# Row factors of the shared key/value norm: from ScalarE's Ln and Exp with a Newton step on VectorE to a power on GpSimd

## The reference, cut to what matters

```python
def rmsnorm(x, g):
    xf = x.astype(jnp.float32)
    y = xf * lax.rsqrt(jnp.mean(xf * xf, axis=-1, keepdims=True) + RMS_EPS)
    return (y * g.astype(jnp.float32)).astype(x.dtype)

def shared_kv(x, norm_kv, w_kv):
    kv = rmsnorm(x, norm_kv) @ w_kv
    k, v = jnp.split(kv, [KV_WIDTH], axis=-1)
```

## Time and profile before

| what | value |
|---|---|
| median of 3 runs | 1838.86 us (1838.41 to 1840.55) |
| the profiled execution's own time | 1838.39 us |
| its span, first to last instruction | 1836.8 us |
| busy share of the span: PE, DVE, ACT, POOL | 95%, 61%, 48%, 14% |
| granted clock of TensorE, mean | 0.986 of full speed |

### The profile page before, as it was taken

How to read it: one execution, slowest core, us unless ns; L and a number is a source line. 1 busy time by engine, 2 the same in 40 slices (tenths; PEclk the granted TensorE clock), 3 DMA queues, 4 the chain that set the end, 5 groups by cost and what they waited for, 6 DMA issues and landing times.

```text
span 1836.8 us, 36758 instructions
## 1 busy us (share of the span) xinstructions
PE 1752.0 (95%) x14273; PEld 1369.2 (75%) x14273; DVE 1113.7 (61%) x2563; ACT 878.0 (48%) x1342; POOL 251.8 (14%) x350
## 2 busy tenths in 40 slices
PE   5999999999999999999999899999999999989996
PEld 4888876677677866677677777877778777778885
DVE  6535646574656546774767776466665676574443
ACT  6545542453343444544244665455555455464442
POOL 1112010131013011121013300210001101001110
PEclk7999999999999999999999999999999999999998
DMA  9423213552255314552254633332223322224432
GB/s 298 141 77 99 70 52 104 149 165 75 58 161 164 81 52 128 162 201 75 67 175 157 220 90 95 100 81 71 77 80 84 99 69 80 75 72 129 115 108 98
DMA packets 270600, 204.53 MB, mean 111 GB/s; under 512 B 8164, under 2 KB 254128, under 8 KB 269184
## 3 DMA queue, kind: packets, MB, share of 16 engines
q1 hardware_dynamic: 251200, 131.71, 25.9%
q0 software_dynamic: 19280, 71.13, 11.4%
HBM read 168.05 MB, written 38.80 MB: 113 GB/s over the span
## 4 chain that ended last, share of the span: by engine, by line
PE 84%; DVE 8%; ACT 3%; issue 2%; DMA 2%; SPq 0%; ACTq 0%; POOL 0%; DVEq 0%; POOLq 0%
PE PP L601 54%; PE PP L850 8%; PE PP L630 3%; PE BS L694 2%; PE B L1040 2%; PE B L725 1%; PE BS L754 1%; PE BS L504 1%; PE B L504 1%; DVE W L1812 1%; PE BS L997 1%; DMA W<-in_w_in_a 1%; PE PP L1133 1%; DVE AR L2042 1%; PE BS L752 1%
## 5 line engine op out<-in xcount | busy, mean ns | idle before, releaser
L601 PE MATMUL PP<-H,W 128*128 128x280 f16 (+1 forms) x8640 | 1055.1, 281 | 8.5 <-DVE W L1812 3.7
L601 PEld LDWEIGHTS PP<-H,W 128*128 128x128 f16 x8640 | 835.0, 98 | 197.7 <-issue 25.2
L1219 ACT ACTIVATE W<-W,SCL 128x1024 f16<-128x1024 f32 x240 | 262.7, 1139 | 333.4 <-DVE SCL L1746 318.8
L1812 DVE SCALAR_TENSOR_TENSOR W<-W,SCL 128x1024 f16<-128x1024 f32 x240 | 307.8, 1292 | 108.5 <-ACT W L1219 104.0
L1208 ACT ACTIVATE wjunk<-W 128x2048 bf16<-128x2048 f32 x120 | 227.7, 1897 | 22.7 <-DMA W<-in_w_in_a 11.0
L850 PE MATMUL PP<-O,W 128*128 128x280 f16 x1536 | 190.5, 284 | 4.8 <-DVE step L1743 4.1
L850 PEld LDWEIGHTS PP<-O,W 128*128 128x128 f16 x1536 | 148.0, 98 | 45.8 <-issue 11.9
L1589 ACT ACTIVATE AR<-AR 128x128 f32<-128x128 f32 x136 | 53.0, 391 | 87.1 <-DVE AR L2343 87.1
L601 PE MATMUL PP<-O,W 128*128 128x280 f16 x576 | 69.6, 282 | 0.5 <-DVE AR L2283 0.5
L1743 DVE TENSOR_SCALAR step<-PP 128x1 f32<-128x1 f32 x107 | 16.5, 154 | 85.3 <-PE PP L531 82.4
L504 PE MATMUL BS<-CST,AR 128*128 128x128 f32 (+3 forms) x318 | 48.4, 273 | 18.8 <-issue 6.5
(11 more groups left out here) (349 smaller groups left out, 1943.9 us busy)
## 6 DMA issues: line engine op xcount, KB each, us to landing
W<-in_w_in_a SPq DMA_DIRECT2D x48, 1024.0 KB, 6.0
W<-in_w_in_b SPq DMA_DIRECT2D x32, 1024.0 KB, 6.0
out<-AR POOLq DMA_DIRECT2D x36, 512.0 KB, 4.7
AR<-in_state_gla POOLq DMA_DIRECT2D x32, 512.0 KB, 5.7
W<-in_w_out_b SPq DMA_DIRECT2D x16, 1024.0 KB, 5.9
W<-in_w_out_a SPq DMA_DIRECT2D x16, 512.0 KB, 5.3
W<-in_w_out_a SPq DMA_DIRECT2D x32, 256.0 KB, 4.0
W<-in_w_kv SPq DMA_DIRECT2D x8, 1024.0 KB, 5.8
```

The source lines that it names most:

```text
L601: last = mm(PP[j % 2][:, c, 0:cols], w[:, k, :], x[:, c * cols:(c + 1) * cols], start=s_, stop=e)
L1219: A(w_parts(j % 2)[0][:, ks], W[:, j % 2, ks], ACT.Copy, scale=SCL[:, j % 4, 0:1]).then_inc(w_hi, 1)
L1812: STT(out=low[:, ks], in0=W[:, j % 2, ks], scalar=SCL[:, j % 4, 0:1], in1=high[:, ks], op0=ALU.mult, op1=ALU.subtract).then_inc(w_ready, 1)
```

## The change

GpSimd forms RB from acc itself, as a power with the exponent -1/2 taken from a column of `small` that DVE sets at the start. It does so in two instructions of 280 columns, each as soon as DVE has that half of acc. ACT's Ln and Exp go, and so do DVE's Newton step and the one-column copy. DVE no longer waits between the two halves of acc. It issues the first low half of the second key unit ahead of its wait for RB (before: between the first tiles of the pair) and then waits for both halves of RB.

```diff
-        ms_done, n_act, n_dve = sem("ms_done"), sem("n_act"), sem("n_dve")
+        ms_done, rb_root, n_dve = sem("ms_done"), sem("rb_root"), sem("n_dve")
...
-            def root(n):
-                act.wait_ge(n_dve, n + 2)
-                A(RB[:], acc[:], ACT.Ln).then_inc(n_act, 1)
-                act.wait_ge(n_act, n + 1)
-                A(RB[:], RB[:], ACT.Exp, scale=-0.5).then_inc(n_act, 1)
-
-            root(0)
             unit_high(kv_unit_at(1), 1)
...
+            V.memset(small[:, 67:68], -0.5)
...
             dve.wait_ge(ms_done, 1)
             cn = Tally(n_dve)
             for c_, b in enumerate((B0, B1)):
-                cn.link(dve, TS(acc[:, c_ * HALF:(c_ + 1) * HALF], b[:, 0:HALF], 1.0 / DM, EPS, ALU.mult, ALU.add))
-            cr = Tally(rs_dve, c.value)
+                cn.inc(TS(acc[:, c_ * HALF:(c_ + 1) * HALF], b[:, 0:HALF], 1.0 / DM, EPS, ALU.mult, ALU.add))
             unit_scale(kv_unit_at(1), 1, 1, B3[:, 300:301])
-            dve.wait_ge(n_act, 2)
-            newton(RB[:], acc[:], x2[:, 0, :], cr)
-            V.tensor_copy(small[:, 66:67], eps_c).then_inc(rb_ready, 1)
+            unit_low(kv_unit_at(1), 1, (0,))
+            dve.wait_ge(rb_root, 1)
+            dve.wait_ge(rb_ready, 2)
...
-                if n in (1, 5):
-                    unit_low(kv_unit_at(1), 1, (n // 5,))
+                if n == 5:
+                    unit_low(kv_unit_at(1), 1, (1,))
...
             residual(0, None, x1T, OUT_A3 // 2, TOK)
+            for c_, done in enumerate((rb_root, rb_ready)):
+                cols = slice(c_ * HALF, (c_ + 1) * HALF)
+                pool.wait_ge(n_dve, c_ + 1)
+                G.tensor_tensor(RB[:, cols], acc[:, cols], small[:, 67:68].broadcast_to([P, HALF]), ALU.pow).then_inc(done, 1)
+            pool.wait_ge(rb_root, 1)
             pool.wait_ge(rb_ready, 2)
             G.memset(acc[:], 0.0).then_inc(acc_zero, 1)
```

## The result

The changed kernel takes 1924.14 us (median of 4 runs, 1917.76 to 1925.31) against 1839.70 us (4 runs, 1838.41 to 1840.96): the ratio is 1.0453, 95% interval 1.0432 to 1.0475. It is 84 us longer, far above the range that ended at 1856 us.

What follows compares the result with a forecast made beforehand. The prediction took the ACT and DVE chain up to the pair's end as the bound, PE waiting for DVE's tiles. Change = 2T - 5.5 us = +0.9 us on 1838.86, so 1839.8 us; range 1835.5 to 1856 us.

Steps and rivals of the forecast that it cites:

- T: Time of one GpSimd power of 128 x 280, forecast at 3.2 us; it counts twice in the change.
- The bound above: Upper end for one GpSimd power of 280 columns: twice eleven passes at 0.69 us each, 15 us.
- geometric middle: Time of one GpSimd power taken as sqrt(0.69 x 15) = 3.2 us, between an add's time and 15 us.
- The third rival: GpSimd's power takes many passes, not overlapped: T = 15, about +25 us, 1864 us; T beyond 11 has chance 0.15.
- The blocking: GpSimd's power holds DVE off, so L1804 and the low half run after both powers: 1.20 + 0.2 us.
- Start: First GpSimd power starts 0.13 us after the first half of acc is done, at 1034.62 us.
- Release: GpSimd's release of DVE after the second power, ahead of the first `normed`: 0.10 us.
- The list: DVE's work from the first `normed` on gets one low half shorter: 1.20 us.
- The floor of 3.4 us: With a quick power, T under 1.75, the low half limits the first `normed`: change -3.4 us, 1835.5 us, chance 0.07.
- The 0 to 2 us: Extra time for PE's pair at half clock after idling, if the power is too slow: 0 to 2 us.
- Slower: Whole kernel slower by more than 0.2%: chance 0.28 + 0.15 = 0.43.

Runs made afterwards that it cites:

- the probes: The kernel before with seven powers that nobody reads, in the stretch where GpSimd waits for the value rows: ratio 1.0006.
- the run with T = 3.67: The changed kernel with the power on 17 of each half's 280 columns and a multiply on the other 263: ratio 0.9996 to the kernel before.

## Why the prediction was wrong

*The step that failed is T, "sqrt(0.69 x 15) = 3.2 us".* It measured 44.98 us, fourteen times as much. The bound above was the worse error: eleven passes for an inverse root, twice for a general power, each at the price of an add, was called a bound and was none. An add costs 0.69 us for 280 columns, so the power costs as much as 65 adds. No row of the trace of before held an operation near it, and a geometric middle between a floor and a guess then stood for knowledge. The third rival (many passes, +25 us at T = 15, a chance of 0.15 beyond T = 11) had the kind right and the size a third of it. The estimate from the Trainium skill (GPSIMD Engine Reference, Performance pitfalls for Q7 kernels), 73 ns a column, was nearer than mine and still less than half of the 160 measured; its 4 cycles a step and my 22 steps together don't account for what a column takes, and which of the two falls short no run here tells.

*The blocking was wrong as well, hidden under the first.* L1798 took 0.23 us and L1806 1.28 us under the first power, VectorE's two-input instructions ran at means of 793 and 739 ns beside the powers of the probes, and the run with T = 3.67 met the sum without the term. An add does hold a low half back: in the timeline of the kernel before, just behind the earlier trace rows, one that started under an add took 1.69 us instead of 1.28.

```profile
1004.34 1.69 DVE L1812 SCALAR_TENSOR_TENSOR W<-W,SCL 128x1024 f16<-128x1024 f32 x1
```

What this and the earlier trace rows show of an add does not hold for a power. So here the measurement speaks against the rule of the Trainium skill (SBUF — State Buffer, Who interferes with whom) as far as it gives the ports to a GpSimd instruction that reads SBUF for its whole length. The powers of the probes, for their part, took 0.3 to 1.2 us more than their columns account for; whether a busy VectorE had a part in that was not tried, nor why a power leaves VectorE free.

*The rest of the sum held.* Start: the power started 0.61 us after acc (0.60 computed). Release: 0.61 + 89.95 + 0.09 = 90.65 us to the first `normed`. The list: from the first `normed` to the third unit 29.74 us against 30.94, 1.20 less, the term of the earlier trace rows. So with T as measured, the terms on record without the blocking give 0.60 + 2 x 44.98 + 0.10 - 6.38 - 1.20 = 83.08 us, against 83.07 measured in the stretch. The floor of 3.4 us was 3.64 with a multiply.

*The clock.* The granted clock fell to 0.50 while PE stood still, and was 0.78 over the first 10 us of the pair, yet the pair took no longer: VectorE's list sets it, and PE's waits took up the loss. PE's group from 1034 to 1153.4 us, beside the earlier trace rows:

```profile
L630 PE MATMUL PP<-O,W 128*128 128x280 f16 x170 | 23.2, 302 | 86.1 <-DVE O L1811 86.1
```

The pair's matmuls took 23.2 us instead of 21.3; the waits behind the first, of 85.03 us here and 0.76 before, were 1.1 us instead of 4.1. The 0 to 2 us that were held ready for it came out at 0.

*The chances.* Slower had 0.43, and the range left out 0.15 above; it ended at T = 11 only because the bound above was taken for one.

## What to carry to other kernels

An operation that the trace does not show is not bounded by counting passes at the price of its neighbours: run it alone first, in a stretch where its engine waits anyway, and read its cost by column, by partition and by instruction. What is right in a change can be had without what is wrong in it: here the early factors gave 3.4 us in the stretch by another function, on an engine that makes them in 0.67 us. And the function table that a stretch leaves behind is part of its cost: here the next loop had to load its own in each of seven rounds.

## What was not expected of the hardware

- GpSimd's power of fp32 takes some 160 ns a column (89.74 us for 560) with 1, 16 or 128 partitions, an exponent of -1/2 or 1 and the bases tried, and 0.2 to 1.2 us more for an instruction; an add takes 2.5 ns a column.
- It does not hold up VectorE's instructions with two SBUF inputs (a low half took 1.28 us under it), as an add does (1.69 us).
- VectorE's reciprocal of 128 x 560 takes 3.65 us, 6.5 ns a column, against 0.74 us for a multiply.
- With 85 us of TensorE idle and its clock at 0.50, the stage behind lost nothing, since another engine set its pace.
